# Each slot of the weight stream loaded by two transfers of 1 MB instead of one of 2 MB

## The reference, cut to what matters

```
def hier_moe(x, w_group, b_group, w_router, b_router, w_gate, w_up, w_down):
    ...
    for e in range(MOE_EXPERTS):
        hdn = jax.nn.silu(t @ w_gate[e]) * (t @ w_up[e])
        y = y + combine[:, e:e + 1] * (hdn @ w_down[e])
    return y.reshape(B, S, D)
```

## Time and profile before

| What | us |
|---|---|
| median of 3 executions | 1764.43 |
| lowest and highest of the 3 | 1761.53, 1765.06 |
| the profiled execution, its own time | 1766.23 |
| span of its profile | 1764.3 |
| TensorE busy in the span | 1575.7 |
| VectorE busy | 541.0 |
| ScalarE busy | 350.9 |

### The profile page before, as it was taken

The page is one execution under the profiler, slowest core; times in us unless marked ns, Lnnn a source line. Parts: engine busy times, 40 slices in busy tenths (PEclk is TensorE's granted clock), DMA queues, the critical chain, the costliest instruction groups (busy, mean ns, idle before and its releaser), DMA issues.

```text
span 1764.3 us, 17040 instructions
## 1 busy us (share of the span) xinstructions
PE 1575.7 (89%) x7298; PEld 885.8 (50%) x7298; DVE 541.0 (31%) x942; ACT 350.9 (20%) x775; POOL 15.1 (1%) x32
## 2 busy tenths in 40 slices
PE   4999988799889999879988998998978998998885
PEld 2677665444358677444435444433324774533332
DVE  1442232621266134352142034121103454211013
ACT  2113230312121323021222122010102242101011
POOL 0000000000000000000000000000002000000000
PEclk8999999789989999978998998899999999899998
DMA  9675452379936623248984522799998333599995
GB/s 383 250 285 192 170 208 99 120 324 421 399 135 271 236 106 136 95 178 336 422 375 100 163 96 101 328 428 427 428 428 337 144 108 131 203 429 428 427 428 229
DMA packets 34760, 463.29 MB, mean 263 GB/s; under 512 B 4432, under 2 KB 4560, under 8 KB 6352
## 3 DMA queue, kind: packets, MB, share of 16 engines
q1 hardware_dynamic: 31568, 447.88, 62.0%
q0 software_dynamic: 3104, 14.15, 2.8%
HBM read 458.87 MB, written 3.15 MB: 262 GB/s over the span
## 4 chain that ended last, share of the span: by engine, by line
PE 78%; DMA 14%; DVE 5%; ACT 2%; issue 1%; SPq 0%; DVEq 0%; ACTq 0%
PE work L641 12%; PE work L481 11%; PE work L697 10%; PE work L472 9%; DMA ring<-in_stream 9%; PE acc L481 6%; DMA area<-in_stream 5%; PE acc L472 5%; PE work L606 5%; PE acc L683 3%; PE work L1105 2%; PE acc L1251 1%; PE work L656 1%; PE acc L793 1%; PE work L904 1%
## 5 line engine op out<-in xcount | busy, mean ns | idle before, releaser
L641 PE MATMUL work<-ring,area 128*64 128x512 f32 x1184 | 265.5, 595 | 29.2 <-DMA ring<-in_stream 29.1
L641 PEld LDWEIGHTS work<-ring,area 128*64 128x64 f32 x1184 | 83.7, 137 | 203.3 <-issue 150.4
L472 PE MATMUL work<-ring,ht_sb 128*128 128x512 f32 (+1 forms) x384 | 148.0, 544 | 5.7 <-ACT ht_sb L1371 2.6
L697 PE MATMUL work<-ring,area 128*64 128x512 f32 x576 | 133.8, 612 | 3.3 <-DVE area L2074 1.7
L481 PE MATMUL work<-ht_sb,ring 128*128 128x256 f32 x576 | 127.6, 381 | 0.0
L481 PEld LDWEIGHTS work<-ht_sb,ring 128*128 128x128 f32 x576 | 108.5, 190 | 18.6 <-issue 3.6
L2111 DVE SCALAR_TENSOR_TENSOR area<-area,comb_slot,work 128x256 f32<-128x256 f32 (+1 forms) x32 | 19.6, 614 | 314.4 <-ACT area L1434 314.2
L481 PE MATMUL acc<-ht_sb,ring 128*128 128x256 f32 x512 | 114.0, 381 | 0.4 <-DMA ring<-in_stream 0.4
L2121 DVE TENSOR_TENSOR area_r<-work,area_r 128x512 fp32r<-128x512 f32 x64 | 44.3, 692 | 217.2 <-ACT area_r L1442 183.9
L472 PEld LDWEIGHTS work<-ring,ht_sb 128*128 128x128 f32 x384 | 74.6, 197 | 71.5 <-issue 62.3
L481 PEld LDWEIGHTS acc<-ht_sb,ring 128*128 128x128 f32 x512 | 96.1, 190 | 17.4 <-issue 4.0
(11 more groups left out here) (272 smaller groups left out, 1734.5 us busy)
## 6 DMA issues: line engine op xcount, KB each, us to landing
ring<-in_stream SPq DMA_DIRECT2D x174, 2048.0 KB, 11.9
area<-in_stream SPq DMA_DIRECT2D x38, 2048.0 KB, 14.0
ln_sb<-in_ln_vecs POOLq DMA_DIRECT2D x8, 1024.0 KB, 7.8
rel_rows<-gain_sb POOLq DMA_DIRECT2D x1, 2048.0 KB, 46.1
area<-rel_rows POOLq DMA_DIRECT2D x16, 128.0 KB, 3.8
cst<-in_consts POOLq DMA_DIRECT2D x1, 1529.5 KB, 9.0
x_sb<-in_x SPq DMA_DIRECT2D x1, 1024.0 KB, 18.3
out_x<-x_sb SPq DMA_DIRECT2D x2, 512.0 KB, 2.6
```

Of the source, the lines that this page charges most:

```text
L472: ins = pe.matmul(dst, src[:, k, t * P:(t + 1) * P], w[:, k, c0:c0 + n], start=k == 0, stop=k == KD - 1)
L641: ins = pe.matmul(banks[half][e * CAP:(e + 1) * CAP, :], tokens[:, k, at:at + CAP], w[:, kk, e, half * W:(half + 1) * W], start=k == 0, st ...
L697: ins = pe.matmul(banks[n][e * CAP:(e + 1) * CAP, :], ACTT[:, f * P + e * CAP:f * P + (e + 1) * CAP], w[:, i, e, n * W:(n + 1) * W], start ...
```

## The change

A function `load_slot` issues two transfers for a slot, one for columns 0 to 2047 and one for columns 2048 to 4095 of every partition, so 8 KB in each partition and 1 MB each. Both raise the same semaphore, by 16 each, and whoever waited for 16 a round now waits for 32 a round. SP's wait for the buffer stands once, before the first of the two. The core of the diff:

```diff
+            def load_slot(s):
+
+                for half in range(2):
+                    part = slice(half * SLOT // 2, (half + 1) * SLOT // 2)
+                    sp.dma_start(slot(s)[:, part], stream[s, :, part]).then_inc(slot_loaded[RING_BANK[s]], 16)
+
...
-            sp.dma_start(slot(0)[:, :], stream[0, :, :]).then_inc(slot_loaded[0], 16)
-            sp.dma_start(slot(1)[:, :], stream[1, :, :]).then_inc(slot_loaded[1], 16)
+            load_slot(0)
+            load_slot(1)
...
                 if nth_round(s) > 1:
                     sp.wait_ge(slot_used[b], nth_round(s) - 1)
-                sp.dma_start(ring[b][:, :], stream[s, :, :]).then_inc(slot_loaded[b], 16)
+                load_slot(s)
...
-            pool.wait_ge(slot_loaded[2], 16 * 2)
+            pool.wait_ge(slot_loaded[2], 32 * 2)
...
             def weights(s):
-                pe.wait_ge(slot_loaded[RING_BANK[s]], 16 * nth_round(s))
+                pe.wait_ge(slot_loaded[RING_BANK[s]], 32 * nth_round(s))
```

More of the change, by code:

```diff
@@ L396, in _ @@
             sp.dma_start(row[:, :], rows).then_inc(first_loaded, 16)
-            sp.dma_start(slot(0)[:, :], stream[0, :, :]).then_inc(slot_loaded[0], 16)
-            sp.dma_start(slot(1)[:, :], stream[1, :, :]).then_inc(slot_loaded[1], 16)
+            load_slot(0)
+            load_slot(1)
             sp.dma_start(X, x.rearrange("(t p) d -> p t d", p=P)).then_inc(inputs_loaded, 16)
             sp.dma_start(vec[:, :], bass.AP(vecs.tensor, 0, [[0, P], [1, N_VECS]])).then_inc(inputs_loaded, 16)
-            sp.dma_start(slot(2)[:, :], stream[2, :, :]).then_inc(slot_loaded[2], 16)
+            load_slot(2)
             for s in range(RING, N_SLOTS):
@@ L1037, in _ @@
                 sa, sbb = SLOTS[f"pa{l}"], SLOTS[f"pb{l}"]
-                pe.wait_ge(slot_loaded[RING_BANK[sa]], 16 * nth_round(sa))
-                pe.wait_ge(slot_loaded[RING_BANK[sbb]], 16 * nth_round(sbb))
+                pe.wait_ge(slot_loaded[RING_BANK[sa]], 32 * nth_round(sa))
+                pe.wait_ge(slot_loaded[RING_BANK[sbb]], 32 * nth_round(sbb))
                 wa = slot(sa)[:, :].rearrange("p (k n) -> p k n", k=4)
@@ L2152, in ada @@
             def ada(s, n):
-                dve.wait_ge(slot_loaded[RING_BANK[s]], 16 * nth_round(s))
+                dve.wait_ge(slot_loaded[RING_BANK[s]], 32 * nth_round(s))
                 if n >= 2:
```

## The result

The changed kernel takes 1770.09 us in the median of 14 executions (1764.84 to 1773.61), the kernel before 1764.45 in 14 beside it. The ratio is 1.0028, with a 95% interval from 1.0018 to 1.0038: slower by 5 us, the interval reaching from 3.2 to 6.7. The forecast was 1770.

A forecast was written before the change was run, and what follows sets the result against it. The stream was taken to bound `moe2` and `moe3`, TensorE `moe0` and `moe1`. 79 slots at 0.070 us gave +5.5 us, other terms 0: 1771.7 on the profiled execution, 1770 on the median, range 1765 to 1775.

The forecast's parts named there:

- The place: `moe2` and `moe3` go at the stream's pace, `moe0` and `moe1` at TensorE's; 38 slots pay in each large stage.
- The price of a packet: In the full stream, 128 more packets a slot cost 70 ns a slot, between 45 and 81, with 0 not excluded.
- the estimate after the Trainium skill: From a stream with 4 KiB rows at 408.7 GB/s: 0.08 us more a slot, 6.3 us in all instead of 5.5.
- The completions: One more completion of a slot on each DMA engine, priced like a small packet at 9 ns.
- How many slots pay: 38 slots in each of `moe2` and `moe3` and three at the start: 79 slots at 0.070 us, 5.5 us.
- SP's issue and the waits: One more 0.33 us issue a slot on SP, and engines waiting for 32 instead of 16: price 0.
- Lone slots: Six slots loaded on a nearly empty queue, from 188.63 to 718.29: put at 0, bounds +0.5 and -2 us.
- a sign of a wrong mechanism: Wrong in kind if the chain's pieces at 188 and 718 change by more than 0.3 us.
- The rival that lone transfers start better: At five lone places and the start, 0.6 us or more saved each: faster by over 3.5 us, about 1760; chance 0.06.
- `moe0` and `moe1`: Stream falls behind 0.2 us more a pair, hidden by early loads: 0; without that cover up to 3.4 us in all.
- That the overlap hides it: Rival: added packets cost only 0 to 45 ns a slot, 0 to +3.5 us, 1764.4 to 1768; chance 0.26.
- That each transfer pays its own fixed time: Rival: up to 2.6 us a slot, up to 205 us; weaker form at seams +9 to +15 us, chance 0.08.

The follow-up runs named there:

- the two runs that divide the slots: Against the changed kernel: two transfers only for slots of `moe2` and `moe3`, 1767.62 us; two only for all other slots, 1762.1 us.
- The run with 4 KB rows: Against the changed kernel, each slot loaded by four column transfers of 512 KB instead of two: 1796.51 us, ratio 1.0174 to the kernel before.
- the run of odd and even partitions: Against the changed kernel, a slot's two transfers split by partition, keeping 16 KB rows: 1764.88 us, ratio 1.0006 to the kernel before.
- the run without the large stages: Against the changed kernel, one transfer for each slot of `moe2` and `moe3`, two for the 116 others: 1762.1 us, ratio 0.9988 to before.

## Why the prediction was right, step by step

*The place* was right: the loss is in `moe2` and `moe3` alone, shown by the two runs that divide the slots and by the gathers of all runs: 5.6 us behind the first of them with the change, none ahead of it.

*The price of a packet* was the term that counts, 70 ns a slot predicted and 75 measured (4.972 against 4.897). Its making was less good than its result. From 4 KB stores, in a window of 1.2 us, and from 16 KB loads I had a busy time of 9 ns a packet beyond its bytes, and 4 ns of overlap, so between 5 and 9 net. The queue in 1220:1300 of the changed kernel shows

```profile
DMA packets 4620, 33.67 MB, mean 421 GB/s; under 512 B 513, under 2 KB 513, under 8 KB 513
...
q1 hardware_dynamic: 4616, 33.61, 101.1%
```

so 1.011 x 16 x 80 = 1294 us, less 513 x 9 ns, over 4103 packets of 8 KB: 314.3 ns. Two of them are 628.6 against 615.7 for one of 16 KB, which is 12.9 ns of busy time and not 9. The overlap was as read: 16 x 314.3 + 2 x 9 = 5047 ns for 4972, 4 ns on each of 18. The net price is 8.9, inside the bounds of 5 and 9; the lower bound had the overlap right and the busy time too small. With the overlap as it is and the busy time as I had read it, a slot would have cost 45 ns and the whole 3.6 us. The 70 ns were a choice between the bounds, with less overlap than I had read, and the two errors met: that the forecast lies within 1 us of the median is in part luck.

The estimate after the Trainium skill ("DMA: Bandwidth & Descriptors", under "iDMA fabric") was 0.08 us a slot, and the trace agrees with 0.075. The run with 4 KB rows gives 2,097,152 bytes in 5.113 us, 410 GB/s, beside the Trainium skill's 408.7.

*The completions*, counted at 9 ns a slot, cost nothing that the run of odd and even partitions could show.

*How many slots pay*: 79 predicted. The three at the start didn't: slot 2 landed at 6.62 + 22.13 = 28.75 against 28.87. The other 76 at 75 ns make 5.7 us, against 5.5 between the two spans.

*SP's issue and the waits* at nothing: right. In the large stages issues were held for up to 1.33 us, against 0.43 in the loop before, with no hole in the full stream. The longest issue of all, 4.38 us at 963 (not 1.35, as an expectation above has it), lies in an attention block and ahead of a gather that came on time.

*Lone slots* at nothing: right so far as it can be told.

```profile
188.55 0.33 SPq L398
188.92 7.38 DMA ring<-in_stream
...
718.44 7.07 DMA ring<-in_stream
```

Both pieces changed by more than the 0.3 us that I had named as a sign of a wrong mechanism, from 7.69 and 7.65. But the chain now counts from the second transfer; from the first issue, at 188.55 and at 718.07, the slots land 7.75 and 7.44 us later, 0.06 more and 0.21 less than before. So the sign was badly chosen. The rival that lone transfers start better isn't shown, and the unexplained 2 us of the run without the large stages leave it not wholly excluded, though the gathers give it nothing.

*`moe0` and `moe1`* at nothing: right. TensorE is busy for 74.00 of 74.00 us there; with 4 KB rows the cover was gone, as that step had said it could be.

*The rivals.* That the overlap hides it fell with 75 ns where it needed 45. That each transfer pays its own fixed time fell with the run of odd and even partitions: 2 transfers, 29.37 us a pair. By the Trainium skill's figure for 1 MB, 341 GB/s ("DMA: Bandwidth & Descriptors", section "Bandwidth"), a slot would have taken 6.15 us, as an estimate; the trace does not agree, the stream of 1 MB transfers here runs at 421 GB/s.

## What to carry to other kernels

When a stream is full, count its packets, not its transfers: here a transfer split across the rows' length paid for each shorter row, and one split across partitions paid nothing. A larger number of transfers is worth having only where somebody starts on the first part. And look first at the lone waits of the engine that bounds the kernel: two waits moved behind the work that didn't need them won four times what the change had lost, three quarters of it accounted for at the two places.

## What the runs showed of the hardware

- A packet on a DMA engine has a price beyond its bytes of about 9 ns in the full stream, for rows of 8 KB (9.4, from 75 ns over 8 packets) and of 4 KB (9.0).
- 16 completions more a slot and an issue of 0.60 us instead of 0.33 left the rate of the full stream where it was, 29.37 us for six slots.
- TensorE's 5.4 us of waiting at the first projection were followed by 5.5 us at a granted clock of 0.53, which cost 2.5 us beyond the wait itself (2.0 at the second).
- With the same instructions and transfers ahead of it, `moe2` was reached 4.2 us earlier in one profiled execution than in another, so a difference of a few microseconds is read from the stage that the change touches, not from the span.
